# First weight chunk in halves over two queues, rope work among the first sums, pooling tables for four groups at once

## What is computed

```python
for i in range(DEPTH):                      # DEPTH = 2
    h = rms_norm(x, norm_g[i])
    proj = h @ w_in[i]                      # 1024 x 9664
    (a_u, a_v, a_z, b_x, b_z, c_q, c_kv, c_kr, c_z,
     d_q, d_k, d_v, d_z, gates) = split(proj)
    y_a = (spatial_gating(a_u, a_v, ...) * silu(a_z)) @ w_a_out[i]
    y_b = (multiscale_pool(b_x, ...) * silu(b_z)) @ w_b_out[i]    # windows 2, 4, 8, 16
    y_c = (latent_attention(c_q, c_kv, c_kr, positions, ...) * silu(c_z)) @ w_c_out[i]
    y_d = (stick_breaking_attention(d_q, d_k, d_v) * silu(d_z)) @ w_d_out[i]
    merged = sum(sigmoid(gates) * (y_a, y_b, y_c, y_d))
    x = x + merged @ w_o[i]
    e = p[i] @ w_ple[i]
    x = x + sigmoid(rms_norm(x, ple_norm_g[i]) @ w_ple_gate[i]) * e
```

## Time and profile before

| | |
|---|---|
| median of 3 executions | 1427.19 us (1424.55 to 1427.26) |
| profiled execution, its own time | 1426.09 us |
| its span, first to last instruction | 1424.3 us |
| PE busy | 1391.0 us, 98% |
| DVE busy | 661.4 us, 46% |
| ACT busy | 562.4 us, 39% |
| POOL busy | 558.5 us, 39% |
| mean granted clock of PE | 0.994 of full |
| mean DMA rate | 90 GB/s |

### The profile page before, as it was taken

How to read it: one execution, slowest core, us unless ns; L and a number is a source line. 1 busy time by engine, 2 the same in 40 slices (tenths; PEclk the granted TensorE clock), 3 DMA queues, 4 the chain that set the end, 5 groups by cost and what they waited for, 6 DMA issues and landing times.

```text
span 1424.3 us, 16230 instructions
## 1 busy us (share of the span) xinstructions
PE 1391.0 (98%) x6592; PEld 1167.5 (82%) x6592; DVE 661.4 (46%) x978; ACT 562.4 (39%) x869; POOL 558.5 (39%) x236
## 2 busy tenths in 40 slices
PE   7979999999999999999999999999999999999998
PEld 6768888888888888888887888888888888888886
DVE  6894454324443332256568654541344443232733
ACT  6444444345453222223543553532544522222241
POOL 4423423343333444444354342424333344444442
PEclk9989999999999999999999999999999999999999
DMA  7212121322222332323343231222222233323232
GB/s 216 78 52 89 60 74 60 89 89 75 84 78 79 98 102 90 107 101 104 90 126 89 65 100 46 94 60 89 89 75 74 74 102 91 104 89 119 91 102 89
DMA packets 75066, 127.61 MB, mean 90 GB/s; under 512 B 8688, under 2 KB 45552, under 8 KB 74992
## 3 DMA queue, kind: packets, MB, share of 16 engines
q1 hardware_dynamic: 74992, 126.57, 29.1%
HBM read 124.45 MB, written 2.10 MB: 89 GB/s over the span
## 4 chain that ended last, share of the span: by engine, by line
PE 91%; DVE 5%; ACT 2%; SPq 1%; issue 1%; DMA 1%; POOL 0%; DVEq 0%; ACTq 0%
PE ps L450 29%; PE ps L452 29%; PE ps L451 29%; SPq L385 1%; PE ps L746 1%; PE ps L703 1%; PE ps L745 1%; DVE n_t L1362 1%; ACT w_hi L907 1%; DMA w_raw<-w_in 1%; DVE pt_lo L1241 0%; PE ps L637 0%; DVE h_lo L1241 0%; DVE vn_lo L1241 0%; DVE xh L1394 0%
## 5 line engine op out<-in xcount | busy, mean ns | idle before, releaser
L425 POOL TENSOR_TENSOR w_lo<-w_raw,w_hi 128x1024 fp32r<-128x1024 f32 x226 | 553.2, 2451 | 815.5 <-ACT w_hi L907 815.3
L450 PE MATMUL ps<-h_hi,w_hi 128*128 128x512 f32 x1088 | 427.1, 393 | 0.0
L452 PE MATMUL ps<-h_hi,w_lo 128*128 128x512 f32 x1088 | 423.8, 390 | 0.0
L451 PE MATMUL ps<-h_lo,w_hi 128*128 128x512 f32 x1088 | 423.4, 389 | 0.0
L907 ACT ACTIVATE w_hi<-w_raw 128x1024 fp32r<-128x1024 f32 (+1 forms) x228 | 239.6, 1052 | 185.0 <-PE ps L452 180.5
L452 PEld LDWEIGHTS ps<-h_hi,w_lo 128*128 128x128 f32 x1088 | 204.2, 188 | 43.1
L451 PEld LDWEIGHTS ps<-h_lo,w_hi 128*128 128x128 f32 x1088 | 204.4, 188 | 41.9 <-issue 0.5
L450 PEld LDWEIGHTS ps<-h_hi,w_hi 128*128 128x128 f32 x1088 | 204.4, 188 | 41.4 <-issue 0.5
L1634 DVE SCALAR_TENSOR_TENSOR m_part<-th,ps 128x512 f32<-128x512 f32 x48 | 33.0, 688 | 236.9 <-PE ps L452 236.8
L1110 ACT ACTIVATE th<-ps 128x512 f32<-128x512 f32 x48 | 28.7, 598 | 192.1 <-PE ps L452 192.1
L450 PE MATMUL ps<-w_hi,act_hi 128*128 128x512 f32 (+1 forms) x192 | 76.4, 398 | 13.9 <-POOL w_lo L425 9.6
(11 more groups left out here) (323 smaller groups left out, 2033.2 us busy)
## 6 DMA issues: line engine op xcount, KB each, us to landing
w_raw<-w_in SPq DMA_DIRECT2D x172, 512.0 KB, 3.6
w_raw<-w_in SPq DMA_DIRECT2D x128, 128.0 KB, 2.5
w_raw<-w_in SPq DMA_DIRECT2D x36, 256.0 KB, 3.0
x<-x_in SPq DMA_DIRECT2D x8, 256.0 KB, 5.0
w_raw<-w_in SPq DMA_DIRECT2D x32, 64.0 KB, 2.2
out_x<-x SPq DMA_DIRECT2D x8, 256.0 KB, 2.1
rows<-rows_in SPq DMA_DIRECT2D x2, 768.0 KB, 5.9
p_raw<-p_in SPq DMA_DIRECT2D x2, 512.0 KB, 4.4
```

The costliest lines, as they stand in the source:

```text
L425: pool.tensor_tensor(w_lo_t[s][:], w_raw_t[s][:], w_hi_t[s][:].bitcast(F32), ALU.subtract).then_inc(w_lo_made, 1)
L450: pe.matmul(o, a_hi, b_hi, start=first, stop=False, skip_group_check=skip)
L451: pe.matmul(o, a_hi, b_lo, start=False, stop=False, skip_group_check=skip)
L452: return pe.matmul(o, a_lo, b_hi, start=False, stop=last, skip_group_check=skip)
```

## The change

- **Loads.** ACT issues the loads of `par` and lat0 itself, on its own queue. SP begins with x0 and x1. The frequencies come in a small tile `freq`, and they and the positions are asked for after x4 instead of last.
- **First chunk in halves.** ACT makes `w_hi` of lat0 in two instructions. DVE makes the first half of its `w_lo`, POOL the second. PE waits for each half apart. ACT's square of x0 comes behind both halves, and DVE's half comes behind its first sum. Each later chunk of lat is made on ACT two x tiles earlier.
- **Idle products.** PE does twelve 128x128 products of ones at once (`wake`), whose result is used by nobody.
- **Rope.** The arguments are made in three parts, behind the sums of tiles 5, 6 and 7, instead of behind `n_r`. PE's rope products stand before av2 instead of behind it, DVE's copies of their results at k=2 instead of k=5 (in both layers).
- **Pooling tables.** The four bands are made first, then one instruction does the edges of all four groups.
- **pt_hi.** The second `keys_high` of a pair stands before two `w_hi` instead of behind them.
- **Tail.** In the last layer DVE finishes tile d before it starts the next.

```diff
 # SP
             load_x(0)
-            sync.dma_start(par[:], par_in).then_inc(par_loaded, 16)
-            load(0, "lat0")
             load_x(1)
...
+            load(0, "lat1")
+            load_x(2)
+            load_x(3)
+            load(0, "lat2")
+            load_x(4)
+            sync.dma_start(freq[:], const_in[:, CC["inv_win"].start:CONSTS]).then_inc(pos_loaded, 16)
+            sync.dma_start(pos_i[:], pos_in.partition_broadcast(P)).then_inc(pos_loaded, 16)
+            load_x(5)
+            load(0, "lat3")
+            load_x(6)
+            load_x(7)
             sync.dma_start(c_st[:], const_in).then_inc(const_loaded, 16)
-            sync.dma_start(pos_i[:], pos_in.partition_broadcast(P)).then_inc(pos_loaded, 16)
 # POOL
+                    if c == 0:
+                        pool.tensor_tensor(w_lo_t[0][:, 4:8, :], w_raw_t[0][:, 4:8, :],
+                                           w_hi_t[0][:, 4:8, :].bitcast(F32), ALU.subtract).then_inc(w_lo_made, 1)
+                        continue
 # PE
+            def wake():
+                pe.wait_ge(ones_made, after(0))
+                for _ in range(12):
+                    pe.matmul(ps[:, 7 * 512:7 * 512 + P], ones[:], ones[:], start=True, stop=True)
...
                 pe.matmul(bank(0), ones[:], n_r[:], start=True, stop=True).then_inc(rb_ready, 1)
+                rope_rows(l)
                 project_rows(l, "av2", 2, hx_hi, hx_lo, 4)
-                rope_rows(l)
 # ACT
+            act.dma_start(par[:], par_in).then_inc(par_loaded, 16)
+            for to, part in gathered(0, "lat0"):
+                act.dma_start(to, part).then_inc(raw_loaded[0], 16)
             act.wait_ge(par_loaded, 16)
             for d in range(KD):
                 act.wait_ge(x_loaded[d], 16)
-                gained(0, d)
-                if d in (0, 3, 5, 7):
-                    weights_up_to(0, f"lat{d // 2}")
+                if d:
+                    gained(0, d)
+                else:
+                    act.activation(tile(act_hi, 0), tile(x, 0), ACT.Copy, scale=col(0, "norm", 0)).then_inc(hx_hi_made, 1)
+                    act.wait_ge(raw_loaded[0], loaded_at[0])
+                    act.activation(w_hi_t[0][:, 0:4, :], w_raw_t[0][:, 0:4, :], ACT.Copy).then_inc(first_hi_made, 1)
+                    act.activation(w_hi_t[0][:, 4:8, :], w_raw_t[0][:, 4:8, :], ACT.Copy).then_inc(w_hi_made, 1)
+                    made[0] = 1
+                    act.activation(n_sq[:, 0, :], tile(x, 0), ACT.Square).then_inc(n_squared, 1)
+                if d in (1, 3, 5):
+                    weights_up_to(0, f"lat{d // 2 + 1}")
...
                 out_high(n, head)
+                keys_high(n + 1, 1)
                 weights_up_to(l, kq, 10)
-                keys_high(n + 1, 1)
 # DVE
             for d in range(KD):
                 gained(0, d)
+                if d == 0:
+                    dve.wait_ge(first_hi_made, after(0))
+                    low(w_lo_t[0][:, 0:4, :], w_raw_t[0][:, 0:4, :], w_hi_t[0][:, 0:4, :]).then_inc(first_lo_made, 1)
+                elif d == 5:
+                    rope_turns()
+                elif d == 6:
+                    rope_rest()
+                elif d == 7:
+                    rope_arguments()
...
-                    if k == 5:
+                    if k == 2:
```

More of the change, by code:

```diff
@@ L462, in project_rows @@
             def project_rows(l, name, i, hi, lo, b, n=SEQ):
-                w_hi, w_lo = chunk(l, name)
+                if number(l, name):
+                    w_hi, w_lo = chunk(l, name)
+                else:
+                    w_hi, w_lo = w_hi_t[0], w_lo_t[0]
                 v_hi = w_hi[:].rearrange("p (k s) c -> p k (s c)", k=2)
@@ L468, in project_rows @@
                     k = 2 * i + u
+                    if number(l, name) == 0:
+                        if u:
+                            pe.wait_ge(w_lo_made, after(0))
+                        else:
+                            pe.wait_ge(first_lo_made, after(0))
                     if name.startswith("lat"):
@@ L1275, in window_tables, with rope_turns @@
                     w = 2 << g
-                    m = tile(window, g, BAND)
-                    settle(dve.tensor_tensor(band[:], u_pad[:, PAD:], u_pad[:, PAD - w:PAD - w + BAND],
-                                             ALU.subtract))
-                    settle(dve.tensor_tensor(edge[:], band[:, 0:PAD],
-                                             c_st[:, CC["inv_edge"].start + g * PAD:CC["inv_edge"].start + (g + 1) * PAD],
-                                             ALU.mult))
-                    settle(dve.tensor_tensor(edge[:], edge[:], e_pad[:, 0:PAD], ALU.subtract))
-                    settle(dve.tensor_copy(tile(edge_hi, g, PAD), edge[:]))
-                    low(tile(edge_lo, g, PAD), edge[:], tile(edge_hi, g, PAD))
-                    settle(dve.scalar_tensor_tensor(m, band[:], 1.0 / w, e_pad[:], ALU.mult, ALU.subtract))
-                dve.sem_inc(windows_made, 1)
-            def rope_arguments():
-                dve.wait_ge(pos_loaded, 16)
+                    last = dve.tensor_tensor(band[:, g, :], u_pad[:, PAD:], u_pad[:, PAD - w:PAD - w + BAND],
+                                             ALU.subtract)
+                settle(last)
+                settle(dve.tensor_tensor(edge[:], band[:, :, 0:PAD],
+                                         c_st[:, CC["inv_edge"]].rearrange("p (g c) -> p g c", g=G), ALU.mult))
+                for g in range(G):
+                    dve.scalar_tensor_tensor(tile(window, g, BAND), band[:, g, :], 1.0 / (2 << g), e_pad[:], ALU.mult,
+                                             ALU.subtract)
+                settle(dve.tensor_tensor(edge[:], edge[:], over(e_pad[:, 0:PAD], [P, G, PAD], 1), ALU.subtract))
+                flat = edge[:].rearrange("p g c -> p (g c)")
+                settle(dve.tensor_copy(edge_hi[:], flat))
+                low(edge_lo[:], flat, edge_hi[:]).then_inc(windows_made, 1)
+            def rope_turns():
+                dve.wait_ge(pos_loaded, 32)
                 settle(dve.tensor_copy(turns[:], pos_i[:]))
-                settle(dve.tensor_scalar(ang[:], turns[:], c_st[:, CC["freq"]], None, ALU.mult))
+                settle(dve.tensor_scalar(ang[:], turns[:], freq[:, G:G + 1], None, ALU.mult))
                 settle(dve.tensor_scalar(turns[:], ang[:], float(1 / (2 * np.pi)), None, ALU.mult))
@@ L1681, in tail, with weighed @@
                     gain_rows(l + 1)
+                def weighed(d):
+                    t = o_t[:, d % 2, :]
+                    dve.wait_ge(gate_tanh, after(n0 + d))
+                    dve.wait_ge(e_taken, after(n0 + KD - 1))
+                    settle(dve.scalar_tensor_tensor(t, t, 1.0, e[:, d, :], ALU.add, ALU.mult))
+                    dve.scalar_tensor_tensor(tile(x, d), t, 0.5, tile(x, d), ALU.mult, ALU.add).then_inc(x_made, 1)
                 for d in range(KD + 2):
```

31 lines of the change are left out of this document (16 added, 15 removed).

## The result

The changed kernel took 1458.8 us (four runs, 1458.5 to 1464.3) against 1427.2 before (1424.6 to 1430.5): ratio 1.0231, interval 1.0211 to 1.025, or 31.5 us slower. The profiled execution took 1458.49, its span is 1456.7, that of before 1424.3. The prediction had 1426.3 and a range that ended at 1430. Some 30 of these us have nothing to do with what the change orders anew: they come from where one new tile of 20 bytes pushed the others.

What follows compares the result with a forecast made beforehand. PE, busy 98% of the span, was taken as the bound, with the change decided in the first 100 us; front +3.2 and later pieces -2.9, -0.65, -0.55 gave -0.9, put at 1426.3 us, range 1420.5 to 1430.

Steps and rivals of the forecast that it cites:

- The pace of the products: Rest of the program after the first 100 us: products the change doesn't touch, so no cost was forecast there.
- all four rivals: DVE not held up, 0.15; POOL's av0 and av1 miss DVE's work, 0.10; late lat0, 0.09; start gains nothing, already in forecast.
- The first chunk's landing: Start of the kernel: lat0 lands at 6.1 us, or about 6.8 if the transfer rate doesn't rise.
- rival (c): Start: two queues share the engines, so lat0 lands late; at 4 us late, 1430.3 us. Chance 0.09, of which 0.06 slower.
- From the landing to the first product: Start: after ACT's halves, n_sq, n_acc and DVE's half, PE starts at 9.4 us instead of 9.57, bounds 9.0 and 10.1.
- The angles among the sums: Layer 0's front: rope work and five POOL hold-ups of DVE end the sums at 33.7 us; PE waits 7 to 9.5.
- From the sums to r_b: Layer 0's front: 16.9 us of PE to av1's end, 1.4 for low clock, 0.9 after n_r; r_b at 53.0, +7.1.
- The stretch on DVE: From r_b's copy to ckvn_lo's end: pooling tables -2.8 us, first two n_t -1.1; front of layer 0 3.2 us longer.
- The later pieces: After layer 0's front: four pt_lo waits gone -2.9 us, layer 1's wait -0.65, the tail -0.55.
- The sum: Whole kernel: 3.2 - 2.9 - 0.65 - 0.55 = -0.9 us.
- the likeliest case: Whole kernel: the forecast itself, 1426.3 us, own range 1423.5 to 1429.5, chance 0.66.
- What was to show it: Right: sums near 33 us after 6 to 9 idle, half clock, ckvn_lo wait near 9; wrong: first product outside 8.5 to 10.5.

Runs made afterwards that it cites:

- the version with the later parts alone: Kernel before plus four-group pooling tables, earlier rope_rows, copies and keys_high, and last-layer sums; old start, rope angles behind n_r, no freq: 1418.2 us, ratio 0.9933.

## Why the prediction was wrong, point by point

**The pace of the products: the step that failed.** "The rest of the program is a wall of products that the change doesn't touch. So what the change is worth is decided in the first 100 us." The change adds no instruction there, and that is all that was looked at. It moves the ring of w_lo by 32 bytes against h_hi, act and w_hi, and the wall grew by 30.5 us. No term of the sum stood for it, nor any rival; all four rivals were about order and waiting. What the runs show in its place: 32 bytes between the tiles make each of these products 5.8 ns longer (226.2 to 232.0), with and without the rest of the change. The diff line was there to be read (`freq` ahead of `window`), and nothing in the trace of before could have given its price: the place of a tile is in no view of the profile. A bound by the nearest rows wasn't sought because the line wasn't taken for a cost at all.

**The first chunk's landing: a term mis-sized.** lat0 was put at 6.1 and landed at 8.7. That was rival (c), held at 0.09: "the two queues share the engines, so that lat0 lands with lat1, x1 and x2 around it". The traces bear it out: SP put x0, x1 and lat1 out by 3.6 and went on, and lat0, wholly issued at 3.2, came with them. On the one queue the same chunk, issued later, is there at 6.0. The Trainium skill's page DMA: Bandwidth & Descriptors, section Issuing engines are not separate DMA queues, says that transfers begun on several engines run on the same 16 DMA engines and interleave, and that only the time to issue is saved; the trace agrees (8.7 us with two queues, 6.0 with one), and the 6.8 us that I had from even sharing was too mild. The 262 against 343 GB/s that I chose between was the lesser matter: in the changed kernel 350 GB/s flowed from 7.0 to 8.0, but not for lat0 alone. (c) decides only from 3.8 us late; lat0 was 2.6 late, and without the new start the kernel was 2.4 us faster.

**From the landing to the first product: right.** Forecast 9.4 with lat0 at 6.1; with lat0 at 6.03 (the run with halves on one queue) it was 9.45, and by the path described, ACT's halves, n_sq, the held-up copy, then DVE's half. That this makes the halves worth next to nothing was right too (9.45 against 9.57 before); that DVE's half has a price at the sums, 1.8 us, was seen only as part of the list. The idle products were done at 6.57, within the 3.5 to 7 forecast, and are worth nothing (0.9999).

**The angles among the sums: right.** From the first product to the sums the forecast had 24.3 us (9.4 to 33.7) and the trace has 24.1 (12.12 to 36.26); PE waited 6.3, forecast 7 to 9.5, since it came later itself. The five hold-ups by GpSimd, under lat1, lat2, lat3, av0 and av1, are all there. That they do harm is shown by the run that undid them, 7.6 us, about the +7.1 by which the first point of the stretch was to move.

**From the sums to r_b: 1.3 us too short.** 19.3 us forecast (33.7 to 53.0), 20.7 in the trace (36.26 to 56.92). Most of it is the low clock after the wait, put at 1.4 us: PE took 19.5 us from the sums to the n_r product (36.26 to 55.76) where it had needed 16.9, 2.6 more. Together with the late chunk r_b comes at +11.0 instead of +7.1.

**The stretch on DVE: nearly right.** r_b's copy to the end of ckvn_lo took 49.05 us (56.92 to 105.97) against 53.66 before: -4.6, forecast -3.9. The parts bear it out: the pooling tables with their stall 4.9 us instead of 7.9 (-2.9, forecast -2.8), the first two n_t 3.08 instead of 3.86 (-0.8, forecast -1.1). With r_b the front is 6.4 us longer, forecast 3.2.

**The later pieces: right.** In the version with the later parts alone, from the ckvn_lo product of layer 0 to that of layer 1 it took 694.95 us against 697.05 (-2.1), from there to the last large product 619.51 against 621.35 (-1.8), and from that to the end 0.5 less: -4.5 together, forecast -4.1. All pt_lo waits are gone, none for kq1 or dv0 came.

**The sum.** With freq out of the way the profiled span is 1.8 us over before's and the ratio 1.0014, where the sum said -0.9; the 1428.3 lies within the likeliest case's own range, 1423.5 to 1429.5. The 2.7 us between the two are r_b, 3.9 later than forecast, less 0.7 in the stretch and 0.4 in the later pieces. The whole miss of 32.5 us is 30.5 of place and 2 of order.

**What was to show it.** The idle time at the sums (7.0 us), the half clock for the first of lat3 (0.50 from 36 to 41), the ckvn_lo wait (8.5) and the missing pt_lo waits were as described; the sums stood at 36.4 and not near 33, the first product at 12.1, beyond the 10.5 that I had named as wrong. None of these signs would have found the 30 us.

## What to carry to other kernels

A tile added or resized ahead of others is a change to every product that reads the tiles behind it. Before costing such an edit, write down the start addresses of all tiles that TensorE reads, before and after, modulo 256 bytes: where they stood alike and no longer do, expect 2 to 3% on each product of 512 columns (693 to 699 ns for three instead of 680), and put the new tile last or fill it up to 256 bytes. In the trace it shows in no wait, only in how many products fit into a window in which PE is full; compare that first when a time grows and the waits don't.

A second queue brings nothing forward by itself: beside a first queue that is kept full, the urgent chunk came 2.6 us later than on that queue in its turn. That it would come early with the rest held back is argued; no run here did that. And work moved ahead of a sum that another engine asks for has to fit in the slack of that sum with the hold-ups counted, 4.0 us here, while the sums came 13.6 us later (22.60 to 36.2).

## What the runs showed of the hardware

- Groups of three products (128x512) take 680 ns where the tiles that TensorE reads start at the same place modulo 256 bytes, and 693 to 699 ns where the low weights' tile is 32, 64, 96 or 128 bytes off; a shift of 256 bytes, or of all tiles together by 32 or 128, costs nothing (1426.5, 1426.5 and 1417.5 us). Of the four, the odd multiples of 32 were worst (1456.6 and 1455.2 us against 1446.3 and 1452.3).
- The shifted tile slows products that don't read it themselves: with w_lo 32 bytes off, those of h_lo and w_hi, during which w_lo is loaded, took 400 ns instead of 389 at 500 to 600 us, and those of h_hi and w_hi, during which w_hi is loaded, 395; those that read w_lo kept their 389. With 64 bytes off it was these that took 398.
- The place of w_raw, which only transfers, ScalarE and GpSimd touch, made no difference (5.44 us a chunk in slot 0 with w_raw 32 bytes off, as before).
- Twelve products of ones, recorded as 24 of some 0.2 us, kept PE busy from 1.08 to 6.57 us; it idled for 5.5 us, and then the first product of 448 columns took 0.74 us as before.
- With two queues feeding, a chunk of 512 KB fully issued at 3.2 us landed at 8.7; on one queue, issued by 3.6, at 6.0.
